# Two-layer hybrid decoder trunk on one NeuronCore: the first value products taken from features before their norm, the position-bias rows added up by GpSimd

## What is computed

```
u = x * rsqrt(mean(x*x, features) + 1e-6) * ln_g[0]
v = u @ w_in[:, 4096:6144]          # values; q, f and gate likewise
f = lb + (1 - lb) * sigmoid(u @ w_f)   # lb from a softmax of hg_lb_logits
o = a gated linear recurrence over chunks of 32 positions, per head of 128
h = x + (rmsnorm(o) * silu(gate)) @ w_out
```

## Time and profile before

| | us |
|---|---|
| median of 3 runs | 1649.3 (1648.06 to 1650.33) |
| the profiled execution, its own time | 1648.23 |
| its span in the trace | 1646.4 |
| PE busy | 1625.8, 99% of the span |
| DVE, ACT, POOL busy | 812.3, 645.4, 20.8 |

### The profile page before, as it was taken

The page is one execution under the profiler, slowest core; times in us unless marked ns, Lnnn a source line. Parts: engine busy times, 40 slices in busy tenths (PEclk is TensorE's granted clock), DMA queues, the critical chain, the costliest instruction groups (busy, mean ns, idle before and its releaser), DMA issues.

```text
span 1646.4 us, 22077 instructions
## 1 busy us (share of the span) xinstructions
PE 1625.8 (99%) x8235; PEld 1387.1 (84%) x8235; DVE 812.3 (49%) x1414; ACT 645.4 (39%) x1096; POOL 20.8 (1%) x40
## 2 busy tenths in 40 slices
PE   7999999999999999999999999999999999999997
PEld 5888888888887998888998888898888889888886
DVE  6674675575677724444333444423344431444445
ACT  4553453453453534333232334332333332243333
POOL 0000000000000000000000000000000000000000
PEclk9999999999999999999999999999999999999999
DMA  6523223323221433333232343333323333433311
GB/s 216 166 78 102 77 76 89 89 77 87 79 77 52 128 90 96 84 84 84 65 115 80 95 97 84 71 102 91 97 66 84 95 71 90 125 94 85 77 51 65
DMA packets 247998, 149.47 MB, mean 91 GB/s; under 512 B 47040, under 2 KB 227648, under 8 KB 247920
## 3 DMA queue, kind: packets, MB, share of 16 engines
q1 hardware_dynamic: 203328, 139.69, 30.6%
q0 software_dynamic: 2608, 8.39, 1.5%
q10 hardware_dynamic: 41984, 0.27, 1.3%
HBM read 146.02 MB, written 6.50 MB: 93 GB/s over the span
## 4 chain that ended last, share of the span: by engine, by line
PE 97%; DVE 2%; ACT 1%; DMA 0%; issue 0%; DVEq 0%; SPq 0%
PE proj L440 81%; PE inner L726 3%; PE inner L440 3%; PE inner L694 2%; PE inner L714 2%; PE inner L682 1%; PE inner L598 1%; PE inner L621 1%; PE inner L624 1%; PE inner L610 1%; PE inner L603 0%; DVE v L1532 0%; PE inner L631 0%; DMA ident<-consts 0%; DVE hT L1140 0%; PE inner L632 0%
## 5 line engine op out<-in xcount | busy, mean ns | idle before, releaser
L1086 DVE TENSOR_TENSOR w_lo<-raw,w_hi 128x1024 fp32r<-128x1024 f32 x252 | 307.8, 1223 | 451.0 <-ACT w_hi L775 449.9
L440 PE MATMUL proj<-u_hi,w_hi 128*128 128x512 f32 x1280 | 509.3, 398 | 0.0
L440 PE MATMUL proj<-u_hi,w_lo 128*128 128x512 f32 x1280 | 499.8, 390 | 0.0
L440 PE MATMUL proj<-u_lo,w_hi 128*128 128x512 f32 x1280 | 498.4, 389 | 0.0
L775 ACT ACTIVATE w_hi<-raw 128x1024 fp32r<-128x1024 f32 x252 | 265.0, 1053 | 127.8 <-PE proj L440 117.0
L440 PEld LDWEIGHTS proj<-u_hi,w_lo 128*128 128x128 f32 x1280 | 240.2, 188 | 52.0
L440 PEld LDWEIGHTS proj<-u_lo,w_hi 128*128 128x128 f32 x1280 | 240.7, 188 | 48.1
L440 PEld LDWEIGHTS proj<-u_hi,w_hi 128*128 128x128 f32 x1280 | 240.5, 188 | 47.8 <-issue 0.4
L440 PE MATMUL proj<-w_hi,u_hi 128*128 128x512 f32 x440 | 177.3, 403 | 3.0 <-DVE u_lo L1106 3.0
L440 PE MATMUL proj<-w_lo,u_hi 128*128 128x512 f32 x440 | 174.6, 397 | 0.0
L440 PE MATMUL proj<-w_hi,u_lo 128*128 128x512 f32 x440 | 174.4, 396 | 0.0
(11 more groups left out here) (172 smaller groups left out, 1490.1 us busy)
## 6 DMA issues: line engine op xcount, KB each, us to landing
raw<-at_w_in SPq DMA_DIRECT2D x160, 512.0 KB, 4.1
raw<-hg_w_in SPq DMA_DIRECT2D x64, 512.0 KB, 4.2
raw<-hg_w_out SPq DMA_DIRECT2D x16, 512.0 KB, 3.6
raw<-at_w_out SPq DMA_DIRECT2D x16, 512.0 KB, 4.8
v<-x SPq DMA_DIRECT2D x4, 512.0 KB, 5.0
bias_tiles<-ext_rows POOLq DMA_DIRECT2D x1, 2048.0 KB, 11.9
bias_tiles<-ext_rows POOLq DMA_DIRECT2D x2, 1024.0 KB, 17.2
bias_n<-bias_tiles POOLq DMA_DIRECT2D x16, 128.0 KB, 4.4
```

The costliest lines, as they stand in the source:

```text
L440: ins = nc.tensor.matmul(bank[:, :], stationary(a), moving(b), start=(first and n == 0), stop=(last and n == 2))
L1086: nc.vector.tensor_tensor(w["lo"][:, slot, :], raw[:, slot, :], w["hi"][:, slot, :].bitcast(F32), ALU.subtract).then_inc(w_ready, 1)
```

## The change

Before, the first value products wait for the norm. In the changed kernel the order of the prologue is another:

- x is multiplied by `ln_g` alone (`x_gain`, DVE), split (`x_high` on ACT, `x_low` on DVE), and the value products are made from that. They go by position tile: a block is 4 feature blocks by one tile of 128 positions, so products begin when the first tile of x is through. The norm factor per position is applied when ACT copies the values (`copy_values` with a scale).
- The copies of the transposes go from DVE to ACT (`x_copy`); of the squares of x only the first stands ahead of them, the others behind the first roundings.
- `norm(0)` still runs, for the heads. It overwrites the same buffers `u_hi` and `u_lo`, so each `u_high` waits for the value products of its pair of blocks, and the first head tile waits for each block of u (`first=True`).
- The splits of tiles 4 to 6 move into `norm(0)`, that of tile 7 behind it; the softmax over `hg_lb_logits` comes after.
- SP loads `ln_g` and weight tile 0 ahead of the tiles 1 to 3 of x.
- PE gets 17 products of ones with ones whose result nobody reads: 7 while it waits for x, 8 and 2 between the first transposes.
- The one-hot matrix and the three products with it are gone. The mask is loaded straight into `ext_sb`, the bias table with heads on 16 partitions (one element at a time), and POOL adds the table's entry to each run of equal buckets: 53 instructions of 1 to 30 elements on 16 partitions. SP waits for the last of them before it stores the rows; DVE's `decays` waits for that store, since `ext_sb` lies in `qx`.

```diff
             load_x(0)
             sp.dma_start(ident[:, :], consts[:, 0:P]).then_inc(const_loaded[0], 16)
+            sp.dma_start(prow[0:16, P:2 * P], ln_g.rearrange("r (h p) -> (r h) p", p=P)).then_inc(const_loaded[3], 16)
+            load(0, *tile_source(HG, 0, "value", 0, 0))
             for t in range(1, ST):
                 load_x(t)
+            for n in range(1, SLOTS):
+                load(n, *tile_source(HG, 0, "value", 0, n))
...
-            sp.dma_start(onehot_sb, onehot).then_inc(const_loaded[5], 16)
-            sp.dma_start(relmask_sb, relmask).then_inc(const_loaded[6], 16)
-            sp.dma_start(relb_sb, rel_bias).then_inc(const_loaded[7], 16)
+            sp.dma_start(ext_sb, relmask).then_inc(const_loaded[6], 16)
+            with nc.allow_non_contiguous_dma("bias table with the heads on partitions"):
+                sp.dma_start(relb_sb, rel_bias.rearrange("b (g h) -> h (b g)", g=GROUPS)).then_inc(const_loaded[5], 16)
...
-                    sp.wait_ge(ext_ready, GROUPS)
+                    sp.wait_ge(ext_ready, 1)
...
+            pool.wait_ge(const_loaded[5], 16)
+            pool.wait_ge(const_loaded[6], 16)
+            for g, bucket, first, count, step in bias_runs():
+                run = slice(g * EXT + first, g * EXT + first + (count - 1) * step + 1, step)
+                ins = nc.gpsimd.tensor_scalar(ext_sb[:, run], ext_sb[:, run],
+                                              relb_sb[:, bucket * GROUPS + g:bucket * GROUPS + g + 1], None, ALU.add)
+            ins.then_inc(ext_ready, 1)
...
                 for k in range(half * KT // 2, (half + 1) * KT // 2):
+                    if first:
+                        pe.wait_ge(u_ready, k + 1)
...
-                if s == 0 and layer is HG:
-                    pe.wait_ge(u_ready, k + 1)
+                if layer is HG and k % 4 == 0:
+                    pe.wait_ge(raw_ready, k + s + 1)
...
+            def x_gain(n):
+                half = n // ST
+                dve.wait_ge(x_copied, n + 1)
+                if n >= 2:
+                    dve.wait_ge(raw_ready, n - 1)
+                nc.vector.tensor_tensor(tmp[:, n % 2, :].rearrange("p (a b) -> p a b", b=P), block(hT, n),
+                                        param[:, 64 + 4 * half:68 + 4 * half].unsqueeze(2).broadcast_to([P, 4, P]),
+                                        ALU.mult).then_inc(xg_made, 1)
+            def x_low(n):
+                dve.wait_ge(raw_hi_ready, n + 1)
+                nc.vector.tensor_tensor(block(u["lo"], n), tmp[:, n % 2, :].rearrange("p (a b) -> p a b", b=P),
+                                        block(u["hi"], n).bitcast(F32), ALU.subtract).then_inc(raw_ready, 1)
...
+            x_square(0)
+            x_copy(0)
+            first_hi(0)
+            x_high(0)
+            x_copy(1)
+            x_copy(2)
+            x_high(1)
+            first_hi(1)
+            x_copy(3)
+            x_high(2)
+            x_high(3)
+            x_square(1)
+            x_copy(4)
+            x_square(2)
+            x_square(3)
```

More of the change, by code:

```diff
@@ L23 @@
+import itertools
 from contextlib import ExitStack
@@ L563, in _ @@
             pe.wait_ge(ones_ready, 1)
+            for _ in range(7):
+                nc.tensor.matmul(proj[2][:, 0:P], ones[:, :], ones[:, :], start=True, stop=True)
             pe.wait_ge(const_loaded[0], 16)
-            for i in range(ST * KT):
-                t, k = i // KT, i % KT
-                if k == 0:
-                    pe.wait_ge(x_loaded[t], 16)
[L569 to L573, removed]
@@ L574, in _, with idle_products, x_transposes @@
-            for i in (1, 2, 3):
-                pe.wait_ge(const_loaded[i], 16)
-            nc.tensor.transpose(proj[0][:, 0:80], prow[0:80, 0:P], ident[0:80, 0:80]).then_inc(param_T, 1)
+            def idle_products(n):
+                for _ in range(n):
+                    nc.tensor.matmul(proj[2][:, 0:P], ones[:, :], ones[:, :], start=True, stop=True)
+            def x_transposes(half, t):
+                n = ST * half + t
+                if half == 0:
+                    pe.wait_ge(x_loaded[t], 16)
+                if n >= 3:
+                    pe.wait_ge(x_copied, n - 2)
+                for i in range(4):
+                    ins = nc.tensor.transpose(inner[1 + n % 3][:, i * P:(i + 1) * P],
+                                              nat[t][:, half, i * P:(i + 1) * P], ident[:, :])
+                ins.then_inc(x_T, 1)
@@ L583, in _ @@
-            for k in range(KT):
-                if k == KT // 2:
-                    bias_rows()
+            for k in (3, 4):
+                for s in range(ST):
+                    value_step(HG, 0, k, s)
+            for i in (1, 2):
+                pe.wait_ge(const_loaded[i], 16)
+            pe.wait_ge(x_copied, 2 * ST)
+            nc.tensor.transpose(inner[1][:, 0:64], prow[0:64, 0:P], ident[0:64, 0:64]).then_inc(param_T, 1)
+            for k in (5, 6, 7):
                 for s in range(ST):
@@ L647, in hg_body @@
                     for half in range(2 * HG.per_head):
-                        head_tile(HG, q, HG.per_head * h + half // 2, half % 2)
+                        head_tile(HG, q, HG.per_head * h + half // 2, half % 2, first=(h == 0 and half < 2))
                         if h:
@@ L810, in _, with block, x_copy, x_high @@
             nc.scalar.preload_act_table_set("natural_log_exp_and_others")
-            for t in range(ST):
+            def block(t, n):
+                half, tile = n // ST, n % ST
+                return t[:, 4 * half:4 * half + 4, tile * P:(tile + 1) * P]
+            def x_copy(n):
+                act.wait_ge(x_T, n + 1)
+                nc.scalar.activation(block(hT, n), inner[1 + n % 3][:, :].rearrange("p (a b) -> p a b", b=P), ACT.Copy)\
+                    .then_inc(x_copied, 1)
+            def x_high(n):
+                act.wait_ge(xg_made, n + 1)
+                nc.scalar.activation(block(u["hi"], n), tmp[:, n % 2, :].rearrange("p (a b) -> p a b", b=P), ACT.Copy)\
+                    .then_inc(raw_hi_ready, 1)
+            def x_square(t):
                 act.wait_ge(x_loaded[t], 16)
                 nc.scalar.activation(spare[t], nat[t], ACT.Square, accum_out=cols[:, t:t + 1]).then_inc(x_squared, 1)
+            x_square(0)
[13 more added lines that the diff above has]
+            x_square(3)
             act.wait_ge(eps_ready, 1)
@@ new lines, in _ @@
+            x_low(0)
+            x_gain(1)
+            x_gain(2)
+            x_low(1)
+            x_gain(3)
+            x_low(2)
+            x_low(3)
+            first_lo(1)
+            x_gain(4)
+            x_gain(5)
+            x_low(4)
+            dve.wait_ge(x_rstd, 1)
+            nc.vector.tensor_tensor(y_f[:, :].rearrange("p (t n) -> p t n", t=ST),
+                                    ident[:, :].unsqueeze(1).broadcast_to([P, ST, P]),
+                                    cols[:, 8:12].unsqueeze(2).broadcast_to([P, ST, P]), ALU.mult)\
+                .then_inc(diag_ready, 1)
@@ L1145, in _ @@
+            x_gain(6)
+            x_low(5)
+            x_gain(7)
+            x_low(6)
+            first_lo(2)
+            x_low(7)
+            first_lo(3)
+            dve.wait_ge(raw_ready, KT)
+            norm(0)
             dve.wait_ge(param_ready, 1)
-            norm(0)
             nc.vector.tensor_tensor(lb[:, :], param[:, 0:H], param[:, H:2 * H], ALU.max).then_inc(lb_step, 1)
@@ L1543, in bucket_of, with distance, bias_runs @@
     return np.where(dist < exact, dist, np.minimum(large, BUCKETS - 1))
+def distance(g, e):
+    window, dilation = ((128, 1), (512, 4), (2048, 16))[g]
+    apart = 2 * P - 1 - e
+    dist = apart * (1 if g == 0 else RES)
+    return dist if apart >= 0 and dist % dilation == 0 and dist <= window else None
+def bias_runs():
+    for g in range(GROUPS):
+        step = RES if g == 2 else 1
+        seen = [e for e in range(EXT) if distance(g, e) is not None]
+        for bucket, run in itertools.groupby(seen, lambda e: int(bucket_of(np.array(distance(g, e))))):
+            run = list(run)
+            assert run == list(range(run[0], run[-1] + 1, step))
+            yield g, bucket, run[0], len(run), step
 def shape_constants():
```

154 lines of the change are left out of this document (80 added, 74 removed).

## The result

The changed kernel takes 1658.45 us (median of 5 runs, 1656.31 to 1660.74) against 1649.3 (1648.06 to 1650.33): 1.0056 times as long, with a 95% interval of 1.0042 to 1.0070. It is slower by 9.2 us, where I had forecast a gain of 4.8. The profiled execution has a span of 1656.8 us, 10.4 more than before.

What follows compares the result with a forecast made beforehand. PE, busy 99% of the span, was taken to bound the kernel, leaving only the prologue to shorten. F's end 5.2 us earlier, less 0.4 for GpSimd beside DVE, gives 4.8: from 1649.3 to 1644.5 us, range 1641.5 to 1649.5.

Steps and rivals of the forecast that it cites:

- F's end: End of head 0's F tile on PE, the yardstick of the gain: at 43.3 us, 5.2 earlier than 48.5.
- the 0.4 for a push on DVE: GpSimd's additions beside DVE's list: 0.4 us taken off the gain, within bounds of nothing and 3.5 us.
- Two sums of the replay: PE's value products after the spreading, 12 then 60, ending at 37.1 us; DVE's norm(0) from 27.8, 14.3 long, to 42.4.
- DVE's list is what is late next: DVE's norm(0) ends at 42.4 us, so PE waits 0.6 to 0.9 in the F tile for a remainder.
- the four value copies (0.6 each) lie on ACT beside this: ACT's value copies ahead of F, hidden beside PE's wait for DVE; each would add 0.6 us without that cover.
- GpSimd's price: The 53 additions on POOL: 0.2 us each, bias rows ready at 29 us and hidden.
- the deadline of 43.5: SP's wait for the bias rows ahead of tile 8's load: additions stay hidden if ready by about 43.5 us.
- break-even at 0.47: POOL's additions: the cover breaks at 0.47 us each, (43.5 - 18.5) / 53.
- The table's landing: DMA of the bias table, 1536 single elements: issued at about 8.7 us, lands behind the full DMA at some 18.5.
- The rival of the slow GpSimd: SP's wait ahead of tile 8: each us behind 43.5 costs one; at 0.75 per addition 1659 us; chance 0.08.
- The rival "GpSimd and DVE hold each other up": DVE's list, 20 to 42 us: pushed by 35 additions, 1647.6 us at 0.10 each, 1651 at 0.2; chance 0.2.
- The clock's rival: PE at 1.2 GHz from 10 to 17 us: products and transposes lose 2.5 us, time 1647; chance 0.08.

Runs made afterwards that it cites:

- e4_store_on_pool_own_place: The changed kernel with the bias rows' store issued by POOL and the rows in a place decays doesn't overwrite: 1643.43 us, ratio 0.9969 to the kernel before.
- e6_memsets: The changed kernel with 53 GpSimd memsets of zeros in place of the additions, so the bias is missing: 1643.72 us against 1648.69, ratio 0.9969.
- e11_values_copied_earlier: e4_store_on_pool_own_place with ACT's copies of the first two value banks ahead of the weight split of tile 6: 1643.49 us against 1648.81, ratio 0.9969.
- e2_gpsimd_only: The kernel before with only the bias rows changed, made by GpSimd's additions: 1651.05 us, ratio 1.0013 to the kernel before.
- e7_own_place_no_idle_products: e4_store_on_pool_own_place without the 17 products of ones: 1644.49 us against 1648.69, ratio 0.9975.

## Why the prediction was wrong

**The prologue was right in its mechanism, and its end nearly so.** First product 10.88 (I said 9.9; ACT could split weight tile 0 at 7.8, which I had landed at 6.6), a wait of 0.8 at 15.9 (about 1 near 14), but for a remainder of the features (`u_lo`, L1223) where I had one of the weights, no wait at the spreading product (half a us), granted clock 1.00 through (as said) with the products 0.23 us apart, F's end 44.6 (43.3). The sum is near what the order and the products are worth once the wait is gone, 4.8 against 5.7 in `e4_store_on_pool_own_place` (5.1 by the ratio). Part of this is luck: F's end, which was to carry it, came 4.0 earlier and not 5.2, the 0.4 for a push on DVE was not there, and 0.6 of what that trace gained lies in the steps behind 584 us.

**Two sums of the replay do not read as they stand.** "Then 12 products to 25.7" and "60 products" count 12 twice: the 37.1 goes with 60 in all behind the spreading, which is what the trace has; read one after the other they would give 39.7. And 27.8 with 14.3 is 42.1, where I wrote 42.4.

**"DVE's list is what is late next"** was right on the list and wrong on the wait. The norm ended at 42.42, and I had said 42.4, so that the 0.3 without a source was right by luck. But PE reached F 1.7 us later than I had it, half of it a wait of 0.83 for ACT to empty a value bank, which I had covered with "the four value copies (0.6 each) lie on ACT beside this". Three of these copies stood in a row on ACT from 37.50 on, behind a weight split. PE never waited for a remainder in F.

**The step that failed** is GpSimd's price, and with it the wait that the forecast put at nothing: "With 1 to 30 elements I take 0.2: ready at 29". Measured: 53 in 32.87 us, 0.62 each, from 19.93 to 52.8, 9.3 behind the deadline of 43.5. SP stood until then, ACT behind it for 9.7 us, and PE for 7.9 and 3.4. I had bounds of 0.10 and 1.09, a nearest row of 0.545 for the same kind of operation on DVE, and a break-even at 0.47 inside them, and chose the value by the memset of 0.10. A memset turned out to be the wrong relative: it reads nothing. Even beside an idle DVE an addition took 0.28, and 0.9 beside a full one. `e6_memsets` shows that with a price like that of the memset the forecast would have held, `e4_store_on_pool_own_place` that with this price it holds once nobody waits.

**The table's landing** was 19.84 rather than 18.5, which is 1.3 of the 9 us between 43.5 and 52.8.

**The rival of the slow GpSimd, to which I gave 0.08, is what happened.** Its place (SP's wait ahead of tile 8) is that of the trace, and so is its threshold of 0.62 each for a loss of over 3.3 us, though the loss that came with it was 9. Its price per us was too low: at 52.8 "each us behind 43.5 delays head 0's chain by a us" gives 9.3, and 14.3 were lost. The rest is, first, that the held-up loads went out in one burst together with the writing of the bias tiles: a median of 8.2 us from issue to landing in the changed kernel between 40 and 80 us, where it was 5.0, and with it the second wait of 3.4. The writing alone is not it, since it lies in the same stretch in the kernel before and in `e4_store_on_pool_own_place`, where the median is 5.0 and 5.1. Second, 3.0 for the clock.

**The rival "GpSimd and DVE hold each other up"** is half right, and that half is the cause of the price. They do not hold each other: DVE's instructions are as long as they were, within 4 ns, and GpSimd alone waits. I took 0.4 for a push on DVE that isn't there, and nothing for the push the other way, which is the one that counts: 0.28 us an addition became 0.9. The Trainium skill ("SBUF — State Buffer", section "SBUF: two separate sides") has the pair: a VectorE instruction with two SBUF inputs stands against a GpSimd one that reads SBUF. The trace agrees for GpSimd (two additions against four, and the additions that end with a DVE instruction, above), and `e6_memsets` agrees on "reads" (53 in 2.06 us, the later half beside DVE instructions with two SBUF inputs and no slower). The page also says that whichever of the two starts first blocks the other; that is not what the rows show, for DVE's mean of 746 to 752 ns for the product with the norm and 685 to 689 for the remainder is the same with and without additions beside it. I had used the page for what it would do to DVE, 1648, and not asked it what DVE does to GpSimd.

**The clock's rival** did not come at its place (1.00 through the prologue); the clock fell only in the stalls, while PE stood.

What stays open: why GpSimd gives way and DVE does not, how much of an addition's wait is its own operand's and how much the table entry's, and what the small steps behind 584 us are that hide the 0.9 us of `e11_values_copied_earlier`.

## What to carry to other kernels

When a break-even lies between the bounds of an unknown price, the time is decided there, and the chance of the bad side is what the bounds say, not what the kindest row says; ask of the row chosen whether it reads and writes the same memories. Before you hand work to a slow engine, look at who waits for its result and what is queued behind that wait: here a store of 72 KB that waited in the queue that feeds the weights cost 9 us, and a buffer shared with the next stage 6, while the work itself could take 40 us unseen once it had its own queue and place. GpSimd's speed on small reads was set by what VectorE did beside it, so put such work where VectorE rests, or don't let its end matter.

## What the runs showed of the hardware

A GpSimd addition on 16 partitions and at most 30 elements, start to start: 0.25 to 0.4 us (mean 0.28) beside an idle VectorE, 0.9 on average beside one full of instructions with two SBUF inputs, up to 2.4 for a single one (`e2_gpsimd_only`). Those over 0.6 us end at most 0.2 us behind the end of a VectorE instruction (all 50 in the changed kernel and `e4_store_on_pool_own_place`). A memset of the same shapes took 0.039, beside an idle VectorE and beside a busy one. A load of 1536 single elements landed 10.7 us after its issue, behind a full DMA. In `e7_own_place_no_idle_products` products stood 0.43 us apart at 11 us although the row gives the granted clock as 1.00 (the column ahead of the DMA share), so at the very start the pace of the products is the better witness:

```profile
11.00:12.00 1.00, 1.00 (x4) 0.71 (x4) 0.45 (x1) 1.00 (x2) 0.00 (x0) 1.00 1.06 406
```
